# Attention of an encoder on one core: probabilities times values for 512 queries at a time

## The chip, the cores and the metric

The kernel runs on one core of a Trainium2 chip. The metric is device time in microseconds (us); the figure before is the median of 3 runs. The engines are named as in the profile: PE is the matrix engine (its weight loads are listed apart, as PEld), ACT the scalar engine, DVE the vector engine, POOL GpSimd, and SP issues the DMAs. Each engine takes its own instructions in program order, and the engines wait for each other through semaphores.

## The reference, cut to what matters

Two layers over 1024 tokens of width 1024. In each, attention with 8 heads stands beside a short convolution, and a projection, an MLP and a gate follow. The change is in attention:

```python
def one_block(args):
    qn_b, qr_b = args
    sc = (jnp.einsum('bqhd,bkhd->bhqk', qn_b, k_nope, preferred_element_type=jnp.float32)
          + jnp.einsum('bqhr,bkr->bhqk', qr_b, k_rope, preferred_element_type=jnp.float32))
    w = jax.nn.softmax(sc * scale, axis=-1)
    return jnp.einsum('bhqk,bkhd->bqhd', w.astype(v.dtype), v)
```

The last line, probabilities times values, is what the change recuts. The sum runs over 1024 keys; there are 64 value columns per head.

## The kernel before, in words

The kernel keeps float32 accuracy by splitting each operand into a high and a low part (`fp32r`) and adding products of the parts. Scores of 128 queries against 1024 keys are one step: a head has 8 steps s = 0 to 7. A step goes through three engines:

1. PE: `score.h.s`, six matmuls 512 wide (L1135 to L1137, tiles kh, hh, kl).
2. DVE: `least.h.s`, a reduction over the 1024 scores (L2386, nm).
3. ACT: `exp.h.s`, the exponential into pr (L1865).
4. PE: `turn.h.s.b`, b = 0 and 1, four transposes each of 128x128 (L1344, ps<-cst,pr) into PSUM bank 4 + b.
5. ACT: `high.h.s.b`, the copy into pth, the high part (L1653, pth<-ps).
6. DVE: `low.h.s.b`, the rest into ptl (L2393).
7. PE: `pv`, the product with the values vv (L1368 and L1369), from pth and ptl. Before, it is done for a quarter of the queries (two steps, 256 columns): `pv.h.G.part`, G = 0 to 3, where part 0 takes key chunks 0 to 3 and part 1 takes chunks 4 to 7. Each part is eight matmuls.

pth and ptl have a first index of 2, so that one quarter can be filled while the other is read.

Around this, PE also makes the next head's keys and values (`kv.1.t`, six matmuls), its queries (`q.1.t`, nine matmuls, on hh and wh or on hh and hl), turns its values by token (`v.1`, L1309) and makes the sums of squares of an output (`var`, L1174 and L1175). ACT and DVE copy, split and normalize these: on ACT `v`, `k` (accy and kh), `out` (of<-ps), `square` (sq<-of), `sq_high` (wh<-sq), `y` (yh<-of); on DVE `q` (tmp or xacc), `q_low` (hl), `sum` and `scale` (of), `sq_low` (wl<-sq,wh), `den` (dent), `y` (yl<-of,yh).

What sets the order is written out by hand: `ATT_PE`, `ATT_ACT` and `ATT_DVE` list the steps of one head for the three engines, and one pass over a list is called a round here. In a name like `turn.0.3.1` the first number is the head relative to the round: -1 is the head before, 1 the next. The change edits `ATT_PE` alone; the lists of ACT and DVE stand as they were. The parts of them that the text speaks of are these:

```python
ATT_ACT: ... exp.0.1 y.-1.0 v.1.0 k.1.0 last.7.1 exp.0.2 high.0.1.0 high.0.1.1 exp.0.3 v.1.1 k.1.1
out.-1.1 high.0.2.0 high.0.2.1 square.-1.1 sq_high.-1.1 unit.0 ...
ATT_DVE: ... sq_low.-1.1 least.0.4 low.0.3.0 low.0.3.1 den.0.0 least.0.5 unit.0 last.6.0 last.7.2
v_turned.1 least.0.6 q.1.0 low.0.4.0 low.0.4.1 scale.-1.1 least.0.7 q_low.1.0 low.0.5.0 low.0.5.1 q.1.1
sum.0.0 low.0.6.0 low.0.6.1 den.0.1 last.7.3 sq_low.0.0 least.1.0 q_low.1.1 low.0.7.0 low.0.7.1 y.-1.1
```

Steps named `last` are only in the round whose head is their first number. Waits that matter: a `turn` needs its `exp` and the `low` of the same b one step earlier (the bank is free then); `v.1` goes into bank 5 and waits for `low.0.3.1`; `kv.1.0` waits for the `ln` of an earlier output; `sq_low` waits for `sq_high`, and `q` on DVE for `q` on PE.

Of the kernel before, what the change touches and what calls it, by code (L numbers as in the profile page):

```python
# [29 lines left out]
HEADS, NOPE, ROPE, V_DIM = 8, 64, 32, 64  # L30
# [180 lines left out]
def steps(text):  # L211

    return [(word.split(".")[0],) + tuple(int(n) for n in word.split(".")[1:]) for word in text.split()]


ATT_PE = steps("""
turn.0.0.0 turn.0.0.1 score.0.2 kv.1.0 score.0.3 turn.0.1.0 turn.0.1.1 pv.-1.3.0 kv.1.1 pv.-1.3.1 turn.0.2.0
turn.0.2.1 score.0.4 pv.0.0.0 turn.0.3.0 turn.0.3.1 score.0.5 pv.0.0.1 var.-1.1 v.1 turn.0.4.0 score.0.6 q.1.0
turn.0.4.1 score.0.7 pv.0.1.0 pv.0.1.1 turn.0.5.0 turn.0.5.1 mix.0.0 q.1.1 turn.0.6.0 turn.0.6.1 mix.0.1
score.1.0 pv.0.2.0 turn.0.7.0 turn.0.7.1 mix.1.0 var.0.0 pv.0.2.1 score.1.1  # L220
""")

ATT_ACT = steps("""
# [243 lines left out]
def encoder(nc, x_in, w_units, w_head, p_in, gains, table, consts, out):  # L467
# [5 lines left out]
    def sb(name, shape, dt, where=ctx):  # L473
        return where.enter_context(nc.sbuf_tensor(name, shape, dt))

    def sem(name):
        return ctx.enter_context(nc.semaphore(name))
# [7 lines left out]
    with ctx:  # L485
# [41 lines left out]
        with ExitStack() as att:  # L527
# [19 lines left out]
            vv = sb("vv", [P, 2, 8, 3 * V_DIM], f32r, att)  # L547
            pth = sb("pth", [P, 2, 8, 256], f32r, att)
            ptl = sb("ptl", [P, 2, 8, 256], f32r, att)
# [23 lines left out]
        ps = ctx.enter_context(nc.psum_tensor("ps", [P, 8, HALF], f32))  # L573
# [98 lines left out]
        t_lo = sem("t_lo")  # L672
        pv_out = sem("pv_out")
# [227 lines left out]
        def step(L, h, s):  # L901

            return (L * HEADS + h) * STEPS + s
# [228 lines left out]
        def _(pe):  # L1132
# [82 lines left out]
            for L in range(DEPTH):  # L1215
# [37 lines left out]
                for n in range(0 if L else SLOTS, len(IN_OUTS) + 1):  # L1253
                    if n < len(IN_OUTS):
                        w, t = IN_OUTS[n]
# [89 lines left out]
                                                   pr[:, s % 2, (4 * b + c) * P:(4 * b + c + 1) * P], ident)  # L1345
                    last.then_inc(t_out, 1)

                def values(h, a, G, part):

                    H = L * HEADS + h  # L1350
                    if part == 0:
                        pe.wait_ge(t_lo, 2 * step(L, h, 2 * G + 2))
                    if (h, G, part) == (0, 0, 0):
                        pe.wait_ge(v_zero, L + 1)
                    if (G, part) == (0, 0):
                        if h + 1 < HEADS:
                            pe.wait_ge(k_lo, H * 2 + 4)
                            pe.wait_ge(v_f, H * 2 + 4)
                        else:
                            pe.wait_ge(o_ln, H * 2 - 1)  # L1360
                    if (G, part) == (2, 0):
                        if h + 1 < HEADS:
                            pe.wait_ge(q_f, H * 2 + 4)
                        else:
                            pe.wait_ge(o_ln, H * 2)
                    dst = ps[:, 6 + G // 2, (G % 2) * 256:(G % 2 + 1) * 256]
                    for c in range(4 * part, 4 * part + 4):
                        nc.tensor.matmul(dst, vv[:, a, c, V_DIM:3 * V_DIM], pth[:, G % 2, c, :], start=c == 0, stop=False)  # L1368
                        last = nc.tensor.matmul(dst, vv[:, a, c, 0:2 * V_DIM], ptl[:, G % 2, c, :], start=False, stop=c == 7)  # L1369
                    if part == 1:  # L1370
                        last.then_inc(pv_out, 1)

                def variances(h, a, t):

# [23 lines left out]
                def attend(h):  # L1398

                    for kind, o, *n in head_steps(h, ATT_PE):  # L1400
                        a, H = o % 2, L * HEADS + h
                        if kind == "turn":
                            transposes(o, *n)
                        elif kind == "score":
                            scores(o, a, *n)
                        elif kind == "kv":
                            if n[0] == 0:
                                if h:
                                    pe.wait_ge(o_ln, H * 2 - 1)
                                else:  # L1410
                                    pe.wait_ge(q_f, H * 2 + 2)
                            else:
                                pe.wait_ge(k_lo, H * 2 + 3)
                                pe.wait_ge(v_f, H * 2 + 3)
                            keys_and_values(o, a, n[0], 6)
                        elif kind == "v":
                            pe.wait_ge(t_lo, 2 * step(L, h, 3) + 2)
                            values_by_token(o, a, 0, 5)
                        elif kind == "q":
                            if n[0]:  # L1420
                                pe.wait_ge(q_f, H * 2 + 3)
                            elif h:
                                pe.wait_ge(o_ln, H * 2)
                            queries(o, a, n[0], 7)
                        elif kind == "pv":
                            values(o, a, *n)
                        elif kind == "mix":
                            mix_first(*n)
                        elif kind == "var" and (o, n[0]) != (HEADS - 1, 1):
                            variances(o, a, n[0])  # L1430
# [215 lines left out]
        def _(act):  # L1646
# [5 lines left out]
            def copy(dst, src, **more):  # L1652
                return nc.scalar.activation(dst, src, ACT.Copy, **more)  # L1653
# [108 lines left out]
            for L in range(DEPTH):  # L1762
# [4 lines left out]
                for n in range(8 if L else 0, len(IN_OUTS)):  # L1767
                    w, t = IN_OUTS[n]
# [100 lines left out]
                def high_of_transposed(h, s, b):  # L1869
                    G = s // 2  # L1870
                    act.wait_ge(t_out, 2 * step(L, h, s) + b + 1)
                    if (h, s, b) == (0, 0, 0):
                        act.wait_ge(tap, L * 12 + 12)
                    if (h, s, b) == (0, 2, 0):
                        act.wait_ge(mix_stored, L * MIX_STORED + 128)
                    if s % 2 == 0 and b == 0 and (G >= 2 or h):
                        act.wait_ge(pv_out, (L * HEADS + h) * 4 + G - 1)
                    copy(pth[:, G % 2, 4 * b:4 * b + 4, (s % 2) * P:(s % 2 + 1) * P],
                         ps[:, 4 + b, :].rearrange("p (c q) -> p c q", c=4)).then_inc(t_hi, 1)

# [51 lines left out]
                def attend(h):  # L1932
                    for kind, o, *n in head_steps(h, ATT_ACT):
                        a = o % 2
                        if kind == "high":
                            high_of_transposed(o, *n)
                        elif kind == "exp":
                            exponentials(o, *n)
                            if (o, n[0]) == (0, 1):
                                high_of_last_conv()  # L1940
                        elif kind == "v":
                            values_by_channel(o, a, n[0], 6)
                        elif kind == "k":
                            keys(o, a, n[0], 6)
                        elif kind == "v_turned":
                            values_by_token(o, a, 0, 5)
                        elif kind == "q":
                            queries(o, a, n[0], 7)
                        elif kind == "out":
                            outputs(o, a, n[0])  # L1950
                        elif kind == "square":
                            output_squares(o, a, n[0])
                        elif kind == "sq_high":
                            high_of_squares(o, n[0])
                        elif kind == "ln":
                            output_ln(o, a, n[0])
                        elif kind == "r":
                            output_factor(o, a, n[0])
                        elif kind == "y":
                            high_of_output(o, a, n[0])  # L1960
                        elif kind == "unit" and o + 2 < HEADS:
                            split_head(L, o + 2, a)
                        elif kind == "last":
                            split_unit(L, O_AT + n[0])
# [843 lines left out]
```

## Time and profile before

| what | before |
|---|---|
| time, median of 3 runs (2713.60 to 2713.67) | 2713.61 us |
| span of the profiled execution | 2712.5 us |
| PE busy | 2698.8 us, 99% |
| DVE busy | 2034.9 us, 75% |
| ACT busy | 1398.9 us, 52% |
| matmuls 256 wide of probabilities and values | 1024 |
| a round of attention, mean of six in the first layer | 34.4 us |

The profiled execution has a span of 2712.5 us from its first to its last instruction; the timed runs are 1.1 us above that. Matmuls are pipelined, and their durations in the profile overlap; what a matmul costs is the distance from its start to the start of the next. A row with x8 is a group of eight instructions merged; its time runs from the first start to the last end.

### The profile page before, as it was taken

To read this page: it belongs to the slowest core of one execution; us is meant where nothing else is said; L and a number is where in the kernel's file an instruction comes from. 1 tells how busy PE (TensorE), PEld (TensorE's weight loads), DVE (VectorE), ACT (ScalarE), POOL (GpSimd) and SP (SyncE) were. 2 spreads that over 40 slices of the span, in tenths; PEclk is the share of its full clock that TensorE was granted. 3 is DMA by queue.
4 is the path that set the end of the run, shared out by engine and by line. 5 is a ranking of instruction groups with operands and counts; after the bars stand their busy time and mean duration, and the time that the engine had idled before them with its cause. 6 is when DMAs were issued, how large, how long until landed. Compare 5 with 4: busy or idle time off the path is not lost.

```text
span 2712.5 us, 34671 instructions
## 1 busy us (share of the span) xinstructions
PE 2698.8 (99%) x12854; PEld 2242.9 (83%) x12854; DVE 2034.9 (75%) x2758; ACT 1398.9 (52%) x2401; POOL 302.7 (11%) x329
## 2 busy tenths in 40 slices
PE   9999999999999999999999999999999999999999
PEld 7888888888888888888888888888888888888886
DVE  5468888476787777798866788893867787777986
ACT  5337888564333333356634478884633333333464
POOL 0230000001111111110003200000011111111000
PEclk9999999999999999999999999999999999999999
DMA  4221112531111111133232111133311111111422
GB/s 166 78 72 37 34 34 76 181 109 71 62 47 55 39 58 51 63 117 117 86 119 73 60 41 34 29 132 131 140 45 49 63 47 55 39 55 55 148 94 78
DMA packets 85943, 206.19 MB, mean 76 GB/s; under 512 B 8976, under 2 KB 37776, under 8 KB 84752
## 3 DMA queue, kind: packets, MB, share of 16 engines
q1 hardware_dynamic: 85776, 203.97, 22.3%
q8 instruction: 103, 1.69, 0.3%
q14 instruction: 64, 0.52, 0.1%
HBM read 172.42 MB, written 31.52 MB: 75 GB/s over the span
## 4 chain that ended last, share of the span: by engine, by line
PE 96%; DVE 2%; ACT 1%; DMA 0%; issue 0%; SPq 0%; ACTq 0%
PE ps L1135 28%; PE ps L1137 28%; PE ps L1136 28%; PE ps L1344 4%; PE ps L1369 2%; PE ps L1368 2%; DVE nm L2386 1%; PE ps L1174 0%; PE ps L1175 0%; DVE ptl L2393 0%; PE ps L1309 0%; PE ps L1202 0%; ACT hh L1653 0%; DVE wl L2147 0%; PE ps L1160 0%; PE ps L1161 0%
## 5 line engine op out<-in xcount | busy, mean ns | idle before, releaser
L1135 PE MATMUL ps<-hh,wh 128*128 128x512 f32 x2160 | 847.9, 393 | 1.4 <-DVE hl L2183 1.3
L1137 PE MATMUL ps<-hh,wl 128*128 128x512 f32 x2160 | 840.8, 389 | 0.0
L1136 PE MATMUL ps<-hl,wh 128*128 128x512 f32 x2160 | 840.7, 389 | 0.0
L1653 ACT ACTIVATE wh<-raw 128x256 fp32r<-128x256 f32 (+2 forms) x510 | 319.2, 631 | 443.2 <-PE ps L1137 314.5
L2147 DVE TENSOR_TENSOR wl<-raw,wh 128x256 fp32r<-128x256 f32 (+2 forms) x510 | 379.6, 757 | 159.0 <-ACT wh L1653 158.6
L1135 PEld LDWEIGHTS ps<-hh,wh 128*128 128x128 f32 x2160 | 405.6, 188 | 89.1 <-issue 3.6
L1136 PEld LDWEIGHTS ps<-hl,wh 128*128 128x128 f32 x2160 | 405.6, 188 | 86.9 <-issue 3.6
L1137 PEld LDWEIGHTS ps<-hh,wl 128*128 128x128 f32 x2160 | 405.5, 188 | 84.5
L2574 DVE TENSOR_TENSOR xf<-xf,ps 128x1024 f32<-128x1024 f32 x280 | 337.4, 1214 | 35.9 <-PE ps L1137 34.7
L1135 PE MATMUL ps<-hx,wh 128*128 128x512 f32 x448 | 174.4, 389 | 0.5 <-DVE xf L2574 0.5
L1137 PE MATMUL ps<-hx,wl 128*128 128x512 f32 x448 | 174.3, 389 | 0.0
L1136 PE MATMUL ps<-hx,wh 128*128 128x512 f32 x448 | 174.3, 389 | 0.0
L2393 DVE TENSOR_TENSOR ptl<-ps,pth 128x512 fp32r<-128x512 f32 x256 | 163.8, 680 | 9.4 <-ACT pth L1653 8.8
L1653 ACT ACTIVATE pth<-ps 128x512 fp32r<-128x512 f32 x256 | 140.5, 595 | 48.2 <-PE ps L1344 45.0
L2386 DVE TENSOR_REDUCE nm<-ps 128x1 f32<-128x1024 f32 x128 | 155.4, 1214 | 1.4 <-PE ps L1137 1.1
L1865 ACT ACTIVATE pr<-ps,nm 128x1024 f32<-128x1024 f32 x128 | 142.8, 1115 | 14.2 <-DVE nm L2386 12.4
L2700 POOL TENSOR_TENSOR spare<-raw 128x256 f32<-128x256 f32 x56 | 43.2, 771 | 872.3 <-DMA raw<-w_units 872.3
L1344 PE MATMUL ps<-cst,pr 128*128 128x128 f32 x1024 | 138.3, 274 | 1.2 <-DVE ptl L2393 1.2
L1344 PEld LDWEIGHTS ps<-cst,pr 128*128 128x128 f32 x1024 | 116.2, 140 | 15.5 <-issue 4.0
L1368 PE MATMUL ps<-pth,vv 128*128 128x256 f32 x512 | 128.1, 284 | 0.0
L1369 PE MATMUL ps<-ptl,vv 128*128 128x256 f32 x512 | 127.2, 283 | 0.0
L1690 ACT ACTIVATE sq<-xf 128x512 f32<-128x512 f32 x168 | 103.1, 623 | 45.0 <-DVE accy L2177 19.8
(241 smaller groups left out, 4303.3 us busy)
## 6 DMA issues: line engine op xcount, KB each, us to landing
raw<-w_units SPq DMA_DIRECT2D x170, 512.0 KB, 3.4
raw<-w_units SPq DMA_DIRECT2D x112, 256.0 KB, 2.9
x_mid<-xf SPq DMA_DIRECT2D x4, 2048.0 KB, 7.9
xf<-x_mid SPq DMA_DIRECT2D x4, 2048.0 KB, 7.7
hh<-mix_hi SPq DMA_DIRECT2D x14, 512.0 KB, 6.1
hl<-mix_lo SPq DMA_DIRECT2D x14, 512.0 KB, 7.0
stage<-w_head SPq DMA_DIRECT2D x16, 320.0 KB, 3.3
mix_hi<-cyh SPq DMA_DIRECT2D x8, 512.0 KB, 2.6
```

What stands on the lines that cost most here:

```text
L1135: nc.tensor.matmul(dst, ah, bh, start=start, stop=False)
L1136: nc.tensor.matmul(dst, ah, bl, start=False, stop=False)
L1137: return nc.tensor.matmul(dst, al, bh, start=False, stop=stop)
L1344: last = nc.tensor.transpose(ps[:, 4 + b, c * P:(c + 1) * P], pr[:, s % 2, (4 * b + c) * P:(4 * b + c + 1) * P], ident)
L1368: nc.tensor.matmul(dst, vv[:, a, c, V_DIM:3 * V_DIM], pth[:, G % 2, c, :], start=c == 0, stop=False)
L1369: last = nc.tensor.matmul(dst, vv[:, a, c, 0:2 * V_DIM], ptl[:, G % 2, c, :], start=False, stop=c == 7)
L1653: return nc.scalar.activation(dst, src, ACT.Copy, **more)
L1865: nc.scalar.activation(pr[:, s % 2, :], ps[:, 2 * (s % 2):2 * (s % 2) + 2, :].rearrange("p b n -> p (b n)"), ACT.Exp, bias=nm[:, s % 2:s % ...
L2147: return V.tensor_tensor(dst, whole, high.bitcast(f32), ALU.subtract)
L2386: V.tensor_reduce(nm[:, s % 2:s % 2 + 1], ps[:, 2 * (s % 2):2 * (s % 2) + 2, :].rearrange("p b n -> p (b n)"), AX.X, ALU.min).then_inc(s_l ...
L2393: V.tensor_tensor(ptl[at], ps[:, 4 + b, :].rearrange("p (c q) -> p c q", c=4), pth[at].bitcast(f32), ALU.subtract).then_inc(t_lo, 1)
L2574: V.tensor_tensor(f, f, ps[:, bank:bank + 2, :], ALU.add if sign > 0 else ALU.subtract).then_inc(down_add, 1)
```

## The change

The product with the values is made for half of the queries (four steps, 512 columns) at a time. `pv.h.t.part` now has t = 0 and 1. There are 512 matmuls of 512 columns where there were 1024 of 256. pth and ptl keep their size, but both of their halves are now read by one product, so they are one buffer of a half and no longer two of a quarter. Part 0 waits for `low` of step 4t+3 with b = 0, part 1 for that with b = 1, and ACT waits with the first `high` of the next half (b = 0 and b = 1 each) until the part that reads the same chunks is done.

```diff
 ATT_PE = steps("""
-turn.0.0.0 turn.0.0.1 score.0.2 kv.1.0 score.0.3 turn.0.1.0 turn.0.1.1 pv.-1.3.0 kv.1.1 pv.-1.3.1 turn.0.2.0
-turn.0.2.1 score.0.4 pv.0.0.0 turn.0.3.0 turn.0.3.1 score.0.5 pv.0.0.1 var.-1.1 v.1 turn.0.4.0 score.0.6 q.1.0
-turn.0.4.1 score.0.7 pv.0.1.0 pv.0.1.1 turn.0.5.0 turn.0.5.1 mix.0.0 q.1.1 turn.0.6.0 turn.0.6.1 mix.0.1
-score.1.0 pv.0.2.0 turn.0.7.0 turn.0.7.1 mix.1.0 var.0.0 pv.0.2.1 score.1.1
+pv.-1.1.0 turn.0.0.0 pv.-1.1.1 turn.0.0.1 score.0.2 kv.1.0 score.0.3 turn.0.1.0 turn.0.1.1 kv.1.1 turn.0.2.0
+turn.0.2.1 score.0.4 turn.0.3.0 turn.0.3.1 score.0.5 var.-1.1 v.1 pv.0.0.0 turn.0.4.0 pv.0.0.1 turn.0.4.1 score.0.6
+q.1.0 score.0.7 turn.0.5.0 turn.0.5.1 mix.0.0 q.1.1 turn.0.6.0 turn.0.6.1 mix.0.1 score.1.0 turn.0.7.0 turn.0.7.1
+mix.1.0 var.0.0 score.1.1
 """)
...
-                def values(h, a, G, part):
+                def values(h, a, t, part):
...
-                    if part == 0:
-                        pe.wait_ge(t_lo, 2 * step(L, h, 2 * G + 2))
+                    pe.wait_ge(t_lo, 2 * step(L, h, 4 * t + 3) + part + 1)
...
-                    dst = ps[:, 6 + G // 2, (G % 2) * 256:(G % 2 + 1) * 256]
+                    dst = ps[:, 6 + t, :].rearrange("p (g n) -> p g n", g=2)
                     for c in range(4 * part, 4 * part + 4):
-                        nc.tensor.matmul(dst, vv[:, a, c, V_DIM:3 * V_DIM], pth[:, G % 2, c, :], start=c == 0, stop=False)
-                        last = nc.tensor.matmul(dst, vv[:, a, c, 0:2 * V_DIM], ptl[:, G % 2, c, :], start=False, stop=c == 7)
-                    if part == 1:
-                        last.then_inc(pv_out, 1)
+                        nc.tensor.matmul(dst, vv[:, a, c, V_DIM:3 * V_DIM], pth[:, :, c, :], start=c == 0, stop=False)
+                        last = nc.tensor.matmul(dst, vv[:, a, c, 0:2 * V_DIM], ptl[:, :, c, :], start=False, stop=c == 7)
+                    last.then_inc(pv_out, 1)
...
-                    if s % 2 == 0 and b == 0 and (G >= 2 or h):
-                        act.wait_ge(pv_out, (L * HEADS + h) * 4 + G - 1)
+                    if s % 4 == 0 and (s or h):
+                        act.wait_ge(pv_out, (L * HEADS + h) * 4 + s // 2 - 1 + b)
```

On PE, at the end of one round and the start of the next, the order before is this: the last score, then all eight transposes of step 0, then the next score and the keys and values (hh with hl in this head), without a value product between them.

```order
L1136 MATMUL ps<-kl,hh 128x512
L1137 MATMUL ps<-kh,hl 128x512
L1344 MATMUL ps<-cst,pr 128x128 x8
L1135 MATMUL ps<-kh,hh 128x512
```

At the same place of the changed kernel, all 16 value matmuls of the head before stand around the first four transposes.

```order
L1137 MATMUL ps<-kh,hl 128x512
L1367 MATMUL ps<-pth,vv 128x512
L1368 MATMUL ps<-ptl,vv 128x512
...
L1344 MATMUL ps<-cst,pr 128x128 x4
L1367 MATMUL ps<-pth,vv 128x512
L1368 MATMUL ps<-ptl,vv 128x512
...
L1344 MATMUL ps<-cst,pr 128x128 x4
L1135 MATMUL ps<-kh,hh 128x512
```

So two value parts now stand ahead of `turn.0.0.1`, `score.0.2` and `kv.1.0`. In the middle of a round, after `var.-1.1`, the order before is `v.1` (L1309), four transposes, a score (kh) and the next head's queries (hh with wh here).

```order
L1309 MATMUL ps<-cst,accy 128x64 x8
L1344 MATMUL ps<-cst,pr 128x128 x4
L1135 MATMUL ps<-kh,hh 128x512
```

In the changed kernel the same place reads so, with eight value matmuls in each of the two groups.

```order
L1309 MATMUL ps<-cst,accy 128x64 x8
L1367 MATMUL ps<-pth,vv 128x512
L1368 MATMUL ps<-ptl,vv 128x512
...
L1344 MATMUL ps<-cst,pr 128x128 x4
L1367 MATMUL ps<-pth,vv 128x512
L1368 MATMUL ps<-ptl,vv 128x512
...
L1344 MATMUL ps<-cst,pr 128x128 x4
L1135 MATMUL ps<-kh,hh 128x512
L1136 MATMUL ps<-kl,hh 128x512
```

Here too two value parts, and `turn.0.4.1` with them, have moved ahead of `score.0.6` and `q.1.0`.

## Rows read from the trace of the kernel before

**Rows 1.** The page: busy time by engine, and the granted clock in 40 slices.

```profile
PE 2698.8 (99%) x12854; PEld 2242.9 (83%) x12854; DVE 2034.9 (75%) x2758; ACT 1398.9 (52%) x2401; POOL 302.7 (11%) x329
...
PEclk9999999999999999999999999999999999999999
```

**Rows 2.** Stretches: six rounds of the first layer, from `turn.0.0.0` to `turn.0.0.0`.

```profile
254.84:461.14 206.30, 206.30 (x1309) 181.84 (x1308) 181.53 (x264) 174.85 (x313) 4.36 (x12) 1.00 0.11 29
```

**Rows 3.** Costliest groups: the high half of the value matmuls.

```profile
L1368 PE MATMUL ps<-pth,vv 128*128 128x256 f32 x512 | 128.1, 284 | 0.0
```

**Rows 4.** Timeline of PE in the second round: start, us, what.

```profile
270.97 0.71 PE L1309 MATMUL ps<-cst,accy 64*128 64x64 f32 x8
271.61 0.66 PE L1344 MATMUL ps<-cst,pr 128*128 128x128 f32 x4
...
273.50 0.39 PE L1135 MATMUL ps<-hh,wh 128*128 128x512 f32 x1
...
275.31 0.39 PE L1137 MATMUL ps<-hh,wl 128*128 128x512 f32 x1
275.55 0.60 PE L1344 MATMUL ps<-cst,pr 128*128 128x128 f32 x4
...
277.37 0.28 PE L1368 MATMUL ps<-pth,vv 128*128 128x256 f32 x1
...
279.30 1.04 PE L1344 MATMUL ps<-cst,pr 128*128 128x128 f32 x8
```

**Rows 5.** Timeline of ACT, second and third round.

```profile
265.92 0.62 ACT L1895 ACTIVATE sq<-of 64x512 f32<-64x512 f32 x1
266.57 0.63 ACT L1653 ACTIVATE wh<-sq 128x512 fp32r<-128x512 f32 x1
...
296.12 1.08 ACT L1653 ACTIVATE pth<-ps 128x512 fp32r<-128x512 f32 x2
297.08 1.13 ACT L1865 ACTIVATE pr<-ps,nm 128x1024 f32<-128x1024 f32 x1
...
298.17 0.62 ACT L1653 ACTIVATE accy<-ps 128x512 f32<-128x512 f32 x1
298.64 0.59 ACT L1653 ACTIVATE kh<-ps 64x512 fp32r<-64x512 f32 x1
299.26 0.59 ACT L1653 ACTIVATE of<-ps 64x512 f32<-64x512 f32 x1
299.88 1.09 ACT L1653 ACTIVATE pth<-ps 128x512 fp32r<-128x512 f32 x2
```

**Rows 6.** Timeline of DVE in the second round.

```profile
275.75 0.69 DVE L2372 SCALAR_TENSOR_TENSOR tmp<-ps,tab 128x512 f32<-128x512 f32 x1 [0.45 <-PE ps L1137]
276.35 1.28 DVE L2393 TENSOR_TENSOR ptl<-ps,pth 128x512 fp32r<-128x512 f32 x2
277.55 0.73 DVE L2418 SCALAR_TENSOR_TENSOR of<-of,gv,sq 64x512 f32<-64x512 f32 x1
278.21 1.21 DVE L2386 TENSOR_REDUCE nm<-ps 128x1 f32<-128x1024 f32 x1
279.34 0.67 DVE L2147 TENSOR_TENSOR hl<-tmp,hh 128x512 fp32r<-128x512 f32 x1
...
285.10 0.20 DVE L2401 STREAM_TRANSPOSE dent<-den 128x32 f32<-128x32 f32 x1
...
285.42 0.68 DVE L2147 TENSOR_TENSOR wl<-sq,wh 128x512 fp32r<-128x512 f32 x1
```

**Rows 7.** Timeline in the first round: PE waits for a `low` of DVE.

```profile
228.54 1.27 DVE L2393 TENSOR_TENSOR ptl<-ps,pth 128x512 fp32r<-128x512 f32 x2
...
229.36 1.23 PE L1344 MATMUL ps<-cst,pr 128*128 128x128 f32 x8 [0.16 <-DVE ptl L2393]
```

**Rows 8.** Timeline: `y` on ACT waits for a store of the part before.

```profile
288.96 0.67 DVE L2147 TENSOR_TENSOR yl<-of,yh 64x512 fp32r<-64x512 f32 x1
...
293.26 0.63 ACT L1653 ACTIVATE yh<-of 64x512 fp32r<-64x512 f32 x1 [1.16 <-DMA mix_lo<-yl]
```

More of the change, by code:

```diff
@@ L1346, in transposes @@
                     last.then_inc(t_out, 1)
-                def values(h, a, G, part):
+                def values(h, a, t, part):
                     H = L * HEADS + h
-                    if part == 0:
-                        pe.wait_ge(t_lo, 2 * step(L, h, 2 * G + 2))
-                    if (h, G, part) == (0, 0, 0):
+                    pe.wait_ge(t_lo, 2 * step(L, h, 4 * t + 3) + part + 1)
+                    if (h, t, part) == (0, 0, 0):
                         pe.wait_ge(v_zero, L + 1)
-                    if (G, part) == (0, 0):
+                    if (t, part) == (0, 0):
                         if h + 1 < HEADS:
@@ L1360, in values @@
                             pe.wait_ge(o_ln, H * 2 - 1)
-                    if (G, part) == (2, 0):
+                    if (t, part) == (1, 0):
                         if h + 1 < HEADS:
```

## Prediction

> **What bounds the kernel now.** I read the page first. PE is busy for 99% of the span, DVE for 75%, ACT for 52%, and the granted clock is in the top tenth in every slice, which is the upper of TensorE's two levels (2.4 GHz) [rows 1]. That says PE, on average. The change is in attention alone, so the stretches come next: six rounds of the first layer take 206.30 us, 34.4 us a round. PE never stops there, but DVE is busy 181.5 us (88%) and ACT 174.9 us (85%) [rows 2], against 75% and 52% over the whole span. So attention is a ring of three engines, nearly full, in which PE ends last. What a change there is worth depends on two numbers for a round: PE's own work, and the longest closed chain of waits through the three hand-written lists. A round cannot be shorter than either. Both follow from starts in the timelines.
>
> **Pitches, from start to start.** A 512-wide product: nine of them take 273.50 to 275.55, 0.228 us each; I take 0.23. A 256-wide value matmul: sixteen from 277.37 to 279.30, 0.1206 us each. `v.1`: 0.64. A half `turn` and a score: 275.55 to 277.37, 1.82, so the half turn alone 1.82 - 6 x 0.23 = 0.44 [rows 4]. The last product of a group reaches its reader 0.44 us after its own start (275.31 to 275.75), 0.21 more than its pitch [rows 4, 6]. ACT: `v` 0.47, `k` at most 0.62 (it may wait there; being the same operation as `v` I take 0.48), `out` 0.62, two `high` 0.96, `exp` 1.09, `square` 0.65, `sq_high` 0.63 and 0.05 to hand it on [rows 5]. DVE: every 512-wide step 0.60, `scale` 0.66, `least` 1.13, `den` 0.32, and 0.67 until a last `low` is done [rows 6]. From the end of a `low` to a waiting PE: the first of the pair is done at 228.54 + 0.67 = 229.21 and PE starts at 229.36, 0.15 [rows 7].
>
> **Part 1: half as many matmuls of twice the width.** Before, a head has 64 value matmuls, 64 x 0.1206 = 7.72 us of PE. After, it has 32; the trace has no value matmul of 512, so I bound it: below by the 0.228 of the products, above by two of 256, 0.241, if the two separate runs of 256 that it reads cost as much as two matmuls. I take 0.23: 32 x 0.23 = 7.36. The gain is 0.36 us a head, 5.8 us over 16 heads (bounds 0 and 6.8). The durations of 284 ns on the page are no help here, since matmuls overlap [rows 3]. The Trainium skill, "TensorE: Matmul & The Clock Gate", section "Back-to-back issue gap", gives N/2.4 + 2.5 ns for an isolated gap: 109.2 ns at 256 and 215.8 ns at 512, an estimate of 2.5 ns saved per pair and 1.3 us in all. Here the row shows 120.6 ns and about 230 ns, so the trace has more to save than the rule. PE's own work in a round becomes 34.4 - 0.36 = 34.0.
>
> **Part 2: what the order does to the chain.** The three lists of steps form this closed chain. I follow it once around in the changed kernel.
>
> A, on PE: `pv.-1.1.0` 1.84 (8 x 0.23), `turn.0.0.0` 0.44, `pv.-1.1.1` 1.84, `turn.0.0.1` and `score.0.2` 1.82, `kv.1.0` 6 x 0.228 = 1.37, tail 0.21: 7.52.
> B, on ACT, which waits for `kv.1.0`: `v` 0.47, `k` 0.48, `exp.0.2` 1.09, `high.0.1` twice 0.96, `exp.0.3` 1.09, `v` 0.47, `k` 0.48, `out.-1.1` 0.62, `high.0.2` twice 0.96, `square` 0.65, `sq_high` 0.68: 7.95.
> C, on DVE, which waits for `sq_high`: `sq_low` 0.60, `least.0.4` 1.13, `low.0.3.0` 0.60, `low.0.3.1` 0.67, to PE 0.15: 3.15.
> D, on PE, where `v.1` waits for `low.0.3.1`: `v.1` 0.64, `pv.0.0.0` 1.84, `turn.0.4.0` 0.44, `pv.0.0.1` 1.84, `turn.0.4.1` and `score.0.6` 1.82, `q.1.0` 2.05, tail 0.21: 8.84.
> E, on DVE, which waits for `q.1.0`: `q` 0.60, `low.0.4` twice 1.20, `scale` 0.66, `least.0.7` 1.13, `q_low` 0.60, `low.0.5` twice 1.20, `q` 0.60, `sum` 0.60, `low.0.6` twice 1.20, `den` 0.32, `sq_low` 0.60, `least.1.0` 1.13, `q_low` 0.60, `low.0.7.0` 0.67, to PE 0.15: 11.26. For `low.0.7.0` the next `pv.-1.1.0` waits, and the chain is closed.
>
> The sum is 38.7 us. Before, the same chain has no value part in it. It closes through `turn.0.0.0`, which waits for that `low` too, so A lacks 3.68; and in D `v.1`, `turn.0.4.0`, `score.0.6` and `q.1.0` follow each other, so D lacks two parts and a half turn, 4.12. That is 38.7 - 7.8 = 30.9 us, 3.5 under the 34.4 that PE takes, which is why it shows nowhere in the profile of before. The change puts all four value parts of a head into it. It then stands 4.7 us over PE's new 34.0, and DVE and ACT sit idle behind PE while value parts run, in a ring that had 12% to spare. The round grows by 38.7 - 34.4 = 4.3.
>
> **Part 3: one buffer.** The new waits of `high` on value parts have little to stop: `high.0.4.0` needs `pv.0.0.0`, which PE does before `turn.0.4.0` anyway, and `high` needs that turn. The same holds for b = 1 and for the next head. Cost zero; the cover is the order of PE itself. If it were gone, a wait here would be at most a part, 1.84.
>
> **The sum.** In each layer, the first head has no value parts ahead of it: its chain is 38.7 - 3.7 = 35.0, and one part stands before the next head's first turn, 36.9, +2.5. Six rounds at +4.3 are 25.8. The last head has no next keys or queries and several other steps in their place; I give it +4.3 too, with 0 and 7.8 (all moved work) as ends. A layer: 32.6; two: 65.2. Added to the span of 2712.5 this is 2777.7, and the timed runs lie 1.1 above the span: 2778.8. The pitches are those of runs without gaps; 0.1 us a round for small ones makes 2780. Nothing behind attention gives it back: MLP and projections wait for attention and keep PE busy as before.
>
> **The rivals.**
> *The gain alone (ends faster).* If the chain had 4.7 us more slack than I sum, PE would stay the bound and only part 1 counts: 2713.6 - 5.8 = 2707.8. It decides from the point where the chain is under 34.0. For it: PE does not wait once in these six rounds. Against it: each link is an order in a list or a wait in the code, and the pitches are the shortest that the rows show. Chance 0.04.
> *Half of it.* Some link is shorter than I read, by 1 to 3 us a round: 14 rounds or so, 2780 less 14 to 42, 2738 to 2766. Chance 0.10.
> *A store joins the chain.* `y.-1.0` on ACT stands before `v.1.0`, and its tile yh is free when the store of the part before has landed: 293.26 - (288.96 + 0.67) = 3.6 us after `y` on DVE [rows 8]. After the change `y.-1.1` follows `low.0.7.1` and ends about 0.8 us before the round's first turn; `y.-1.0` comes 0.44 + 1.84 + 0.64 + 0.48 + 1.09 = 4.5 after that turn (the turns, the part between them, the way to ACT, one `high`, one `exp`). So 5.3 - 3.6 = 1.7 us are left, less what the store waits in SP's queue behind the transfer of the sums. If that makes it 2 us too late, five heads in each layer pay: +20, 2800. Chance 0.07.
> *The clock falls.* PE now idles in pieces of up to about 1 us, 12% of a round. In the trace of before the granted clock stays at the upper level through PE's waits in the first round [rows 7, 1]. If it fell to 1.2 GHz for one round, its 34 us of PE work would take up to twice as long: 2814 and more. The Trainium skill, same page, section "What's actually happening", says that the clock is throttled unless PE is kept busy; by that rule a sparser PE is at risk. Chance 0.03.
> *The forecast.* Chance 0.76, with 2765 to 2798 as its own range: `k` at 0.62 twice a round adds 4 us, the 512-wide value matmul at 0.241 adds 5, the last head moves it by -9 to +7, and each handoff that is off by 0.05 moves it by less than 1 a link.
>
> **The numbers.** 2780. The range of 2758 to 2802 takes in most of the half case and the store. A difference of 0.2% (5.4 us) is about what can be told from no change. Slower by more: forecast, store, clock and half together, 0.95, of which I take off 0.01 for the unforeseen; the gain alone is just at the bound for faster, 0.04; 0.02 is left for the same.
>
> **What would show it.** In the profile after, the six rounds from the first `turn.0.0.0` to the seventh take 6 x 38.7 = 232 us, PE idles for 4.7 us of each (less in the listed waits, since modelled ends hide some 0.16 each time), and the releasers are `low` steps (ptl): before `v.1` (L1309) about 1 us, and before turns (L1344) and `pv.-1.1.0`. PE must wait for ACT hardly anywhere. Value matmuls have a pitch of 0.23. MLP stretches are unchanged. The forecast is wrong if PE idles at `v.1` and nowhere else, if the waits are put down to a DMA, or if the pitch of value matmuls is near 0.24 or above.

## The result, and the profile after

| | before | after |
|---|---|---|
| time, median | 2713.64 us | 2790.21 us (2789.11 to 2790.75) |
| ratio | | 1.0282 (1.0269 to 1.0295) |
| span of the profiled execution | 2712.5 us | 2787.3 us |

The change makes the kernel 76.6 us slower; 2780.0 was predicted, with 2758 to 2802 as the range. The page of the kernel after, its busy times, granted clock and the engines of the chain that ended last, and below it the line of that chain before:

```profile
PE 2726.1 (98%) x12342; PEld 2206.2 (79%) x12342; DVE 2036.7 (73%) x2758; ACT 1398.5 (50%) x2401; POOL 303.0 (11%) x329
...
PEclk9999999999999999999999999999999999999999
...
PE 85%; DVE 8%; ACT 5%; issue 2%; DMA 0%; SPq 0%; ACTq 0%
```

```profile
PE 96%; DVE 2%; ACT 1%; DMA 0%; issue 0%; SPq 0%; ACTq 0%
```

From [rows 1] to these lines the busy shares hardly move: PE was busy for 99% of the span and is for 98%. The chain that ended last does: it now runs through DVE and ACT for 13%, for 3% before. Busy shares alone give no reason for 75 us. Where they are is told by the first and the last transpose of probabilities (L1344) of each layer. The columns are least, median and largest ns, and first and last start. First the two layers before, then after:

```profile
L1344 PE MATMUL ps<-cst,pr x512: 270/272/329, 220.7 to 489.3; 128*128 128x128 f32 x171
L1344 PE MATMUL ps<-cst,pr x512: 270/273/329, 1563.9 to 1832.4; 128*128 128x128 f32 x171
```

```profile
L1344 PE MATMUL ps<-cst,pr x512: 270/273/447, 220.5 to 524.8; 128*128 128x128 f32 x171
L1344 PE MATMUL ps<-cst,pr x512: 270/273/303, 1601.0 to 1905.5; 128*128 128x128 f32 x171
```

Attention of the second layer took 268.5 us from first to last transpose and takes 304.5, +36.0; the first layer goes from 268.6 to 304.3, +35.7. From the last transpose of the second layer to the end of the span it was 880.1 us and is 881.8; behind the first layer's there are 1.7 us more as well, some 0.9 of them value work that now stands behind the last transpose. So attention has it all, and convolution, projections and MLP give nothing back. The six rounds that [rows 2] measured before:

```profile
256.69:493.74 237.05, 218.09 (x1117) 167.53 (x1116) 182.11 (x264) 174.88 (x312) 4.35 (x12) 1.00 0.09 25
```

They took 206.30 us and take 237.05: 39.5 a round for 34.4. DVE and ACT do the same work (182.1 and 174.9 us) in more time, and PE, which has no idle time in the row before, idles for 19 us. What it waits for in the whole kernel (us in total, times, longest):

```profile
PE ps L1344 <- DVE ptl L2391: 29.2, 41, 2.0
PE ps L1309 <- DVE ptl L2391: 9.5, 14, 0.8
PE ps L1174 <- DVE wl L2145: 3.7, 14, 0.3
PE ps L1367 <- DVE ptl L2391: 3.3, 15, 0.2
...
PE ps L1135 <- ACT pr L1863: 0.8, 2, 0.4
```

Nearly all is `low` (ptl), as said ahead. The chain can be followed through one round. PE, from the start of link A to the start of link D:

```profile
294.01 0.50 PE L1367 MATMUL ps<-pth,vv 128*128 128x512 f32 x1 [0.22 <-DVE ptl L2391]
294.35 0.39 PE L1368 MATMUL ps<-ptl,vv 128*128 128x512 f32 x1
...
295.73 0.40 PE L1368 MATMUL ps<-ptl,vv 128*128 128x512 f32 x1
295.96 0.60 PE L1344 MATMUL ps<-cst,pr 128*128 128x128 f32 x4
...
298.26 0.60 PE L1344 MATMUL ps<-cst,pr 128*128 128x128 f32 x4
...
309.36 1.23 PE L1344 MATMUL ps<-cst,pr 128*128 128x128 f32 x8 [1.34 <-DVE ptl L2391]
...
313.12 0.71 PE L1309 MATMUL ps<-cst,accy 64*128 64x64 f32 x8 [0.70 <-DVE ptl L2391]
```

ACT and DVE in the same round, where the chain passes to them:

```profile
301.66 0.60 ACT L1651 ACTIVATE accy<-ps 128x512 f32<-128x512 f32 x1 [0.29 <-PE ps L1137]
302.16 0.58 ACT L1651 ACTIVATE kh<-ps 64x512 fp32r<-64x512 f32 x1
302.76 1.11 ACT L1863 ACTIVATE pr<-ps,nm 128x1024 f32<-128x1024 f32 x1
...
309.39 0.63 ACT L1651 ACTIVATE wh<-sq 128x512 fp32r<-128x512 f32 x1
```

```profile
310.05 0.69 DVE L2145 TENSOR_TENSOR wl<-sq,wh 128x512 fp32r<-128x512 f32 x1 [0.24 <-ACT wh L1651]
...
320.04 1.22 DVE L2384 TENSOR_REDUCE nm<-ps 128x1 f32<-128x1024 f32 x1 [3.05 <-PE ps L1137]
322.10 0.69 DVE L2370 SCALAR_TENSOR_TENSOR tmp<-ps,tab 128x512 f32<-128x512 f32 x1 [0.84 <-PE ps L1137]
```

Each bracket is one engine that waits for the one before it in the chain. DVE alone idles for 3.05 and 0.84 us behind PE here, while the two value parts after `v.1` run. So the round grows although no engine has more work. The links against the prediction:

| link | predicted, us | measured, us |
|---|---|---|
| A, PE, 294.01 to 301.66 | 7.52 | 7.65 |
| B, ACT, to 310.05 | 7.95 | 8.39 |
| C, DVE, to 313.12 | 3.15 | 3.07 |
| D, PE, to 322.10 | 8.84 | 8.98 |
| E, DVE, to the next value part, 333.78 | 11.26 | 11.68 |
| sum | 38.7 | 39.8 |

### The profile page after: what moved, and what is told of

Same layout as the page of the kernel before. It is cut to its first block, busy times and chain, and to the rows that moved or that the text cites. A ratio compares the mean times of both kernels' runs of the same rounds, so it can differ in the third digit from the quotient of the medians.

```text
span 2787.3 us, 33647 instructions
## 1 busy us (share of the span) xinstructions
PE 2726.1 (98%) x12342; PEld 2206.2 (79%) x12342; DVE 2036.7 (73%) x2758; ACT 1398.5 (50%) x2401; POOL 303.0 (11%) x329
## 4 chain that ended last, share of the span: by engine, by line
PE 85%; DVE 8%; ACT 5%; issue 2%; DMA 0%; SPq 0%; ACTq 0%
PE ps L1135 26%; PE ps L1137 26%; PE ps L1136 26%; DVE ptl L2391 2%; PE ps L1367 2%; PE ps L1368 2%; DVE nm L2384 2%; ACT pr L1863 1%; ACT pth L1651 1%; PE ps L1344 1%; DVE wl L2145 1%; ACT wh L1651 1%; DVE hl L2145 1%; ACT sq L1893 0%; ACT of L1651 0%
## 5 line engine op out<-in xcount | busy, mean ns | idle before, releaser
L1344 PE MATMUL ps<-cst,pr 128*128 128x128 f32 x1024 | 151.7, 277 | 31.8 <-DVE ptl L2391 29.2
L1344 PEld LDWEIGHTS ps<-cst,pr 128*128 128x128 f32 x1024 | 114.7, 140 | 83.8 <-issue 69.7
L1367 PE MATMUL ps<-pth,vv 128*128 128x512 f32 x256 | 106.3, 415 | 3.3 <-DVE ptl L2391 3.3
L1135 PE MATMUL ps<-kh,hh 128*128 128x512 f32 x256 | 108.2, 423 | 1.1 <-ACT pr L1863 0.8
```

What stands on the lines that cost most here:

```text
L1135: nc.tensor.matmul(dst, ah, bh, start=start, stop=False)
L1344: last = nc.tensor.transpose(ps[:, 4 + b, c * P:(c + 1) * P], pr[:, s % 2, (4 * b + c) * P:(4 * b + c + 1) * P], ident)
L1367: nc.tensor.matmul(dst, vv[:, a, c, V_DIM:3 * V_DIM], pth[:, :, c, :], start=c == 0, stop=False)
```

## The experiments

Theories: **order** (the closed chain of PE's new order, as predicted), against **buffer** (one buffer in place of two makes `high` wait for value parts) and **width** (the 512-wide matmul costs more than two of 256). Rounds below are the distance from one `v.1` to the next in the first layer; it is 34.4 us before and 39.5 after. Where an expectation speaks of walking the lists, every engine is stepped through its list with the pitches of the rows and the waits of the code, and the length of a round is read from that.

### The order alone, narrow and with two buffers

The kernel before, with the parts where the change puts them. Nothing else is edited.

```diff
 ATT_PE = steps("""
-turn.0.0.0 turn.0.0.1 score.0.2 kv.1.0 ... pv.-1.3.0 kv.1.1 pv.-1.3.1 ...
+pv.-1.2.0 pv.-1.2.1 turn.0.0.0 pv.-1.3.0 pv.-1.3.1 turn.0.0.1 score.0.2 kv.1.0 ...
...
+var.-1.1 v.1 pv.0.0.0 pv.0.0.1 turn.0.4.0 pv.0.1.0 pv.0.1.1 turn.0.4.1 score.0.6 q.1.0 ...
```

> The kernel before (256-wide value matmuls, pth and ptl as two buffers of a quarter, its waits) with the changed kernel's order on PE: each value part of 512 columns is replaced by the two parts of the quarters that it covers. Chain theory (the order on PE puts the value parts into the closed chain of waits): PE makes the same stops as in the changed kernel. The chain that I can sum for this kernel closes one link later (pv.-1.3.0 waits for low.0.7.1) and comes to 37.3 us a round at least, walking all three lists with the pitches of the rows gives 38.7; so 2755 to 2790, likeliest 2780. Buffer theory (what costs is that one buffer of a half makes ACT wait for the value parts): with two buffers back, the time returns to about 2714, 2720 at most. Width theory (what costs is the 512-wide matmul over two runs): 2714 as well.

Measured: 2785.70 us (2784.68 to 2786.40), ratio 1.0264 (1.0249 to 1.028), rounds 39.25. Nothing wide and no shared buffer is in it, and the loss is 72.1 of the 76.6 us. Buffer and width fall as its cause. Its waits have the same shape as those after:

```profile
PE ps L1344 <- DVE ptl L2393: 29.7, 41, 2.0
PE ps L1309 <- DVE ptl L2393: 9.5, 14, 0.8
PE ps L1174 <- DVE wl L2147: 3.7, 14, 0.3
```

### One of the two moves alone

Only the parts at the start of a round are moved, and then only those of the middle.

```diff
+pv.-1.2.0 pv.-1.2.1 turn.0.0.0 pv.-1.3.0 pv.-1.3.1 turn.0.0.1 score.0.2 kv.1.0 ...
```

> The kernel before with only the last two quarters' value parts of the head before moved to the start of the round, around turn.0.0.0 (as in the changed kernel); the middle of the round stays as before. Chain theory: only 3.9 us of value parts join the chain; walking the lists gives 35.7 us a round instead of 34.4 and 2736 (2725 to 2750) in all. Buffer or width theory: 2714. If every moved part cost alike, without a threshold: half of the 77 us, 2752.

Measured: 2743.74 us (2742.53 to 2744.72), ratio 1.011 (1.0095 to 1.0125), rounds 35.8 and 36.5 in turn.

```diff
+var.-1.1 v.1 pv.0.0.0 pv.0.0.1 turn.0.4.0 pv.0.1.0 pv.0.1.1 turn.0.4.1 score.0.6 q.1.0 ...
```

> The kernel before with only the first two quarters' value parts moved behind v.1, around turn.0.4.0, and turn.0.4.1 ahead of score.0.6 (as in the changed kernel); the start of the round stays as before. Chain theory: 3.9 us of value parts and a half turn join the chain; walking the lists gives 36.6 to 37.3 us a round and 2752 to 2758 (2740 to 2770). Buffer or width theory: 2714. Start and middle together should come near the 70 to 77 us that both cost.

Measured: 2755.02 us (2754.26 to 2755.25), ratio 1.0151 (1.0136 to 1.0166), rounds 37.0 and 37.2. The two cost 30.2 and 41.4 us, 71.6 together, and 72.1 when made at once. If they lengthened two separate chains, the round with both would be the longer of the two, 37.1; it is 39.25. So with both made, both are links of one chain. But a chain of 30.9 with one move alone, 3.9 us of narrow parts at the start or 4.3 with the half turn in the middle, would have given 34.8 and 35.2, and 36.2 and 37.1 were measured. Of these 1.4 and 1.9 us the sum lacks 0.8 with both moves too (38.7 for 39.5). And if the two ate up the slack of one chain, together they would cost more than the sum of each alone, where they cost the same. So the slack of 3.5 us before is a sum and was not measured. Walking the whole lists had given 35.7 for the start and 36.6 to 37.3 for the middle. With one move alone the parts that stay at their old places (`pv.0.0.0` ahead of `turn.0.3.0`, and so on) stand in a way round too; the runs don't show which.

### Other orders of PE, the other lists as they are

In the changed kernel one part goes ahead of `v.1`, so that one link holds for `low.0.3.0` and not for `low.0.3.1`.

```diff
-... score.0.5 var.-1.1 v.1 pv.0.0.0 turn.0.4.0 pv.0.0.1 turn.0.4.1 ...
+... score.0.5 var.-1.1 pv.0.0.0 v.1 turn.0.4.0 pv.0.0.1 turn.0.4.1 ...
```

> The changed kernel with one step moved: pv.0.0.0 goes ahead of v.1 instead of behind it, so that PE does it in the time in which v.1 waits for low.0.3.1 (pv.0.0.0 itself waits for the low before that one). Chain theory: the chain loses the part of the 1.84 us that fits into PE's stop, 0.6 us a round: 2782 (2778 to 2786). Buffer and width theory: no change, 2790, since the same parts and waits remain.

Measured: 2783.81 us (2783.37 to 2784.43), ratio 1.0258 (1.0244 to 1.0272), rounds 39.07. Of the chain 0.4 us a round are gone, where 0.6 were expected of that link, and no more; buffer and width would have left it at 2790. The next one is the best order for PE that was found for the wide parts by walking the lists with the pitches of the rows, the lists of ACT and DVE untouched.

```diff
-... kv.1.1 turn.0.2.0 turn.0.2.1 score.0.4 turn.0.3.0 turn.0.3.1 score.0.5 var.-1.1 v.1 pv.0.0.0 turn.0.4.0 ... q.1.0
+... kv.1.1 score.0.4 turn.0.2.0 turn.0.2.1 score.0.5 turn.0.3.0 turn.0.3.1 var.-1.1 pv.0.0.0 q.1.0 v.1 turn.0.4.0 ...
```

> The changed kernel with the best order of PE's own list that I found by walking the lists, the lists of ACT and DVE untouched. Chain theory: PE's order alone can't take the value parts out of the chain, since all queries' turns of a half must come ahead of them and the fixed lists of ACT and DVE put the rest behind; 38.3 us a round, 2778 (2770 to 2786). If the changed order on PE were just badly chosen, a better one would bring it to 2720 or less.

Measured: 2782.52 us (2781.80 to 2783.06), ratio 1.0253 (1.0236 to 1.027). PE's list alone does not mend it.

### The lists of ACT and DVE alone

The changed kernel with PE's order as the change has it, and new lists for ACT and DVE.

```diff
 ATT_ACT = steps("""
-high.0.0.0 high.0.0.1 exp.0.1 y.-1.0 v.1.0 k.1.0 last.7.1 exp.0.2 high.0.1.0 high.0.1.1 exp.0.3 v.1.1 k.1.1
-out.-1.1 high.0.2.0 high.0.2.1 square.-1.1 sq_high.-1.1 ...
+high.0.0.0 y.-1.0 exp.0.1 out.-1.1 high.0.0.1 last.7.1 square.-1.1 sq_high.-1.1 v.1.0 k.1.0 exp.0.2 high.0.1.0
+...
+ln.-1.1 last.7.2 r.-1.1 exp.0.5 high.0.4.0 y.-1.1 out.0.0 high.0.4.1 square.0.0 sq_high.0.0 exp.0.6 ...
 ATT_DVE = steps("""
-scale.-1.0 low.0.0.0 low.0.0.1 ... y.-1.0 k.1.1 sum.-1.1 low.0.2.0 low.0.2.1 sq_low.-1.1 least.0.4 ...
+scale.-1.0 low.0.0.0 y.-1.0 sum.-1.1 low.0.0.1 ... low.0.4.0 sum.0.0 low.0.4.1 least.0.6 sq_low.0.0 y.-1.1 q.1.0 ...
+... low.0.7.0 low.0.7.1 den.0.1 least.1.1 q_low.1.1
```

> The changed kernel with its own order on PE and its one buffer, and only the lists of ACT and DVE put in another order, so that the steps on which PE's next stop waits come ahead of those that have time (found by walking the lists). Chain theory: the same matmuls, the same waits of high on value parts, but no closed chain above PE's work: 34.3 us a round, 2722 (2712 to 2735). Buffer theory: the waits of high on the value parts remain, so the time stays near 2790. Width theory: also near 2790.

Measured: 2769.29 us (2766.35 to 2770.57), ratio 1.0202 (1.0188 to 1.0216), rounds 37.6 to 39.6 from the second on: a miss. In the six rounds ACT's longest waits are for a DMA, which holds it five times:

```profile
ACT pth L1650 <- PE ps L1343: 20.1, 32, 1.4
ACT yh L1650 <- DMA mix_lo<-yl: 17.5, 5, 4.0
```

One such wait, on ACT and in SP's queue:

```profile
335.11 0.63 ACT L1650 ACTIVATE yh<-of 64x512 fp32r<-64x512 f32 x1 [3.36 <-DMA mix_lo<-yl]
```

```profile
328.93 1.26 SPq L1064 DMA_DIRECT2D sums<-dent  x4
331.08 0.47 SPq L1073 DMA_DIRECT2D sq<-sums  x1
331.59 0.60 SPq L1056 DMA_DIRECT2D mix_hi<-yh  x1
332.23 0.60 SPq L1056 DMA_DIRECT2D mix_lo<-yl  x1
```

The store of yl stands in SP's queue behind the transfer of the sums and was issued at 332.23, and `y.-1.0` on ACT, now early in the list, could start only at 335.11. `exp.0.1` and `k.1.0` stand behind it on ACT; in the same six rounds PE waits five times each for kl of DVE (8.3 us) and for pr of ACT (4.7 us). A part of the miss can be the clock: its mean over the profiled span is 0.995, by which some 14 of 2769 us of full clock are missing, less what PE would have waited anyway. The waits for the DMA are the rival "a store joins the chain". It is not in the changed kernel, where ACT waits for DMAs of weights only, but in a version of it that shortens the chain elsewhere. I had left SP's queue out of the walk. With it in, and `y` and `den` placed so that the store has time (`y.-1.1` on DVE behind `sq_low.0.0` of the round's end, `den.0.1` ahead of `low.0.6.0`):

```diff
 ATT_ACT = steps("""
+exp.0.1 y.-1.0 high.0.0.0 out.-1.1 high.0.0.1 last.7.1 square.-1.1 sq_high.-1.1 v.1.0 k.1.0 exp.0.2 high.0.1.0
+...
+ln.-1.1 r.-1.1 last.7.2 exp.0.5 y.-1.1 high.0.4.0 out.0.0 square.0.0 high.0.4.1 exp.0.6 q.1.0 high.0.5.0
 ATT_DVE = steps("""
+scale.-1.0 y.-1.0 low.0.0.0 sum.-1.1 low.0.0.1 ... low.0.4.0 sum.0.0 least.0.6 low.0.4.1 q.1.0 ...
+q.1.1 den.0.1 low.0.6.0 low.0.6.1 sq_low.0.0 y.-1.1 low.0.7.0 last.7.3 least.1.0 least.1.1 low.0.7.1 q_low.1.1
```

> Second try at the changed kernel with only the lists of ACT and DVE reordered. In the first try y on ACT waited up to 4.0 us for the store of the part before, which stands in SP's queue behind the transfer of the sums (den.0.1); with that store put into the walk, it gives the 37.5 us a round that the first try showed. This order gives the store its time. Chain theory: 34.5 us a round by the walk, 2724 (2716 to 2735), with PE's order and the one buffer of the changed kernel as they are. Buffer or width theory: near 2790. If the first try's shortfall had another cause than the store, this one stays at 2760 or more.

Measured: 2731.51 us (2730.07 to 2733.85), ratio 1.0066 (1.0052 to 1.008), rounds 34.9. PE executes the changed order to the letter, with one buffer and wide matmuls, and 58.7 of the 76.6 us are back. So the loss belongs to neither PE's order nor ACT's and DVE's by itself: it is what the three lists cost together. The last round, where several steps are others, loses still; the longest wait there is 2.83 us for ptl. The mean granted clock of 0.998 can be some 5 us of the 17.9 that are left.

### All three lists, wide and narrow

The changed kernel with three new lists, and the same lists with 256-wide parts and two buffers, to read the width where PE ends last.

```diff
 ATT_PE = steps("""
-pv.-1.1.0 turn.0.0.0 pv.-1.1.1 turn.0.0.1 score.0.2 kv.1.0 score.0.3 ... v.1 pv.0.0.0 turn.0.4.0 pv.0.0.1 ... q.1.0
+pv.-1.1.0 kv.1.0 score.0.2 pv.-1.1.1 turn.0.0.0 turn.0.0.1 score.0.3 ... q.1.0 pv.0.0.0 v.1 turn.0.4.0 score.0.6 pv.0.0.1 ...
 ATT_ACT = steps("""
+exp.0.1 v.1.0 y.-1.0 last.7.1 k.1.0 out.-1.1 high.0.0.0 high.0.0.1 exp.0.2 square.-1.1 sq_high.-1.1 ...
 ATT_DVE = steps("""
+scale.-1.0 least.0.2 y.-1.0 k.1.0 last.7.1 sum.-1.1 low.0.0.0 low.0.0.1 least.0.3 sq_low.-1.1 ... low.0.7.0 ... low.0.7.1
```

> The changed kernel with all three lists (PE, ACT, DVE) in another order, found by walking the lists. Chain theory: PE is the bound again, with 0.36 us less work a head than before: 33.9 us a round by the walk, where the kernel before walks at 34.3; 2708 (2704 to 2715), faster than both. Buffer or width theory: 2760 or more.

> Control for the run with all three lists in another order: the same ACT and DVE lists and the same places on PE, but with the 256-wide value matmuls and two buffers of the kernel before. If what makes the wide one faster than before is the width, this one lies 5 to 6 us above it, at 2713 (2709 to 2718); if it is the order, both are alike.

Measured: wide 2712.47 us (2712.20 to 2713.42), ratio 0.9995 (0.9986 to 1.0004), rounds 34.2: inside the expected 2704 to 2715, but not the expected gain on the kernel before. Narrow 2716.49 us (ten of eleven executions lie from 2716.10 to 2717.15; one took 11415.86, for which no reason is on record), ratio 1.001 (1.0001 to 1.0019), rounds 34.5. At these lists the width, with the one buffer, is worth 4.0 us by the times, and 0.3 us a round. The page of the wide one:

```profile
PE 2694.1 (99%) x12342; PEld 2210.1 (82%) x12342; DVE 2035.0 (75%) x2758; ACT 1399.2 (52%) x2401; POOL 299.9 (11%) x329
...
PE 95%; DVE 4%; ACT 1%; issue 0%; DMA 0%; SPq 0%; ACTq 0%; DVEq 0%
```

A second set of lists, with the two transposes of a step drawn apart and `kv.1.0` first in the round:

```diff
 ATT_PE = steps("""
+kv.1.0 pv.-1.1.0 turn.0.0.0 score.0.2 pv.-1.1.1 turn.0.0.1 turn.0.1.0 score.0.3 kv.1.1 turn.0.1.1 turn.0.2.0 ...
```

> The changed kernel with all three lists reordered once more, from the order that gave 2712.5, with the store in the walk. Chain theory: 33.9 us a round as there, and 1 to 1.5 us less per layer in the first and the last head: 2710 (2707 to 2713).

Measured: 2713.76 us (2713.36 to 2714.28), ratio 0.9999 (0.999 to 1.0008): outside the expected 2707 to 2713, and no gain. Its rounds are 34.1, 0.25 under those before, which would be 3.5 us in 14; it is not seen in the time. Its longest waits on PE (us in total, times, longest):

```profile
PE ps L1343 <- DVE ptl L2390: 2.7, 4, 0.8
PE ps L1343 <- ACT pr L1862: 1.9, 2, 1.0
PE ps L1134 <- DVE xacc L2369: 1.7, 2, 0.9
```

They happen four, two and two times in the whole kernel, so in single rounds; that the lists serve the first and the last round less well is the likely reason, and it was not tested. No version beats the kernel before by more than can be told; the best of them is level with it.

## Why the prediction was right, step by step

- **What bounds: right.** A round is the longer of PE's own work and the closed chain. The change makes the chain longer, with the six rounds in full: 237.05 us for 232 predicted. The stops are where they were said to be: ptl before `v.1` (0.70 us for 1), before turns and before `pv.-1.1.0`, and ACT hardly holds PE (0.8 us in all). PE's idle time in the profile is 3.2 us a round, not 4.7; as foretold, modelled ends hide a part of each stop. What is not shown is the other half of the argument, that the chain had 3.5 us of slack before: one move alone costs more than that allows.
- **Part 2, the mis-sized term.** The chain was summed to 38.7 and takes 39.5 on average, so the six rounds cost 30.7 and not 25.8 a layer. Of the 1.05 us missing in the round shown, B has 0.44 and E 0.42. In B, `k` costs 0.60 and 0.62 to the next start where I took 0.48, although [rows 5] had 0.62 for it; I put that down to a wait, because the operation's name is the same as for `v`. That is 0.26 of the 0.44, and the own range of the forecast had named it (4 us, for 0.62 twice a round). Most of the rest of B is 0.15 at the square, which starts 1.11 us after the pair of pth, for 0.96. Neither is a fixed price of its shape. In the round before this one, after the change, the same `k.1.0`, with the same tiles, takes 0.48:

```profile
262.90 0.58 ACT L1651 ACTIVATE kh<-ps 64x512 fp32r<-64x512 f32 x1
263.38 1.10 ACT L1863 ACTIVATE pr<-ps,nm 128x1024 f32<-128x1024 f32 x1
```

Here the exponential starts 0.10 us before the end of `k`, and at 302.76 above 0.02 behind it. The square comes 0.97 after the pair in that round. What decides between the two was not tested, nor what the small pieces of E are.
- **First and last head: right.** +2.1 and +2.5 for the two first heads (2.5 predicted); 4.5 for each last one (4.3), 2.9 of it up to the last transpose and 1.7 behind it.
- **Part 1, the width.** Predicted 5.8 us with bounds of 0 and 6.8; the pair of runs with the same lists measures 4.0. The pitch is as taken: the seven from 294.35 to the transpose at 295.96 take 1.61 us, 0.230 each. Under the changed order the width gains nothing at all: the wide kernel is 4.5 us slower than the narrow one with that order. A fall of the clock explains about 1.7 of it (last section). For the rest there is a reading that no run tested: the first wide part needs both steps of its half, so it waits for `low.0.7.0` in 15 rounds (3.3 us in the waits), while in the narrow kernel the first quarter needs only earlier steps and starts right behind the score:

```profile
332.66 0.39 PE L1137 MATMUL ps<-kh,hl 128*128 128x512 f32 x1
332.89 0.28 PE L1368 MATMUL ps<-pth,vv 128*128 128x256 f32 x1
```

- **Part 3, the buffer at zero: right as far as tested.** Order and narrow parts alone give 72.1 of 76.6 us, and the second run with new lists keeps the one buffer and comes to within 17.9 us of the kernel before; with all lists, it is level. No wait of `high` for a value part has a row of its own in the waits of after.
- **The rivals.** The gain alone (2707.8) did not come; the version with all lists gets near it at 2712.47. Half of it did not come; the error had the other sign. The store is not in the change and did appear in the first run with new lists. The clock fell once, for a few us and not for a round.

## What to carry to other kernels

Before moving work within one engine's list, close the chain: from the moved step through every engine's queue back to itself, at the pitches of the rows, and compare the sum with the busiest engine's own work. A full engine that never waits can hide a chain with little slack, and here 7.8 us of matmuls moved into one with, by the sum, at most 3.5 to spare. When only a part of the work moves, other ways round count too, and the one chain summed too little. When the work must move, the lists of the other engines have to move with it, DMA queues among them; take the pitch of an operation from its own rows, at each place where it stands, not from another with the same name.

## What the runs showed of the hardware that was not expected

**The same stop, and another clock.** At the end of attention in the first layer PE stops for 2.01 us, and right afterwards it runs at the lower level, 1.2 GHz. The kernel after, timeline and then the stretch:

```profile
502.99 1.68 PE L1344 MATMUL ps<-cst,pr 128*128 128x128 f32 x8 [2.01 <-DVE ptl L2391]
...
505.32 0.63 PE L1137 MATMUL ps<-kh,hl 128*128 128x512 f32 x1
505.75 0.63 PE L1135 MATMUL ps<-kh,hh 128*128 128x512 f32 x1
```

```profile
503.00:507.00 4.00, 4.00 (x15) 3.25 (x16) 2.94 (x5) 3.30 (x7) 0.53 (x1) 0.57 1.00 402
```

The narrow kernel with the changed order, at its own copy of the place:

```profile
501.08 1.23 PE L1344 MATMUL ps<-cst,pr 128*128 128x128 f32 x8 [2.02 <-DVE ptl L2393]
```

```profile
503.00:507.00 4.00, 3.38 (x20) 2.47 (x19) 3.63 (x6) 3.15 (x7) 0.00 (x0) 1.00 1.03 422
```

In the first the pitch of a 512-wide matmul is 0.43 us in place of 0.23 and the mean granted clock of those 4 us is 0.57, which is 1.7 us of full clock lost; in the second a stop as long leaves the clock at 1.00. So does the stop at the same place of the second layer in the kernel after itself, where the 512-wide matmul keeps its 0.23:

```profile
1883.75 1.23 PE L1344 MATMUL ps<-cst,pr 128*128 128x128 f32 x8 [2.01 <-DVE ptl L2391]
...
1885.05 0.39 PE L1136 MATMUL ps<-kl,hh 128*128 128x512 f32 x1
1885.28 0.40 PE L1137 MATMUL ps<-kh,hl 128*128 128x512 f32 x1
```

With the start alone moved, the clock fell behind both stops of 2.02 us. In the first run with new ACT and DVE lists alone it fell after a stop of 1.63 us (at 380.2), not after an equal one (at 303.5), and was below 1.00 in eight stretches of 10 us over the kernel. What decides was not found, so here a stop of 1.6 to 2 us is to be counted as a risk of 1.7 us on top. The Trainium skill, "TensorE: Matmul & The Clock Gate", section "What's actually happening", says the clock is throttled unless PE is kept busy; the first case agrees, and the second shows that a stop of 2.02 us alone is not enough to bring it down. The same page, section "Wait — 56ns, not 53.3ns?", gives 426.7 ns from start to start for 512 columns at the lower level and 215.7 ns at the upper: the trace agrees with the first (0.43) and not with the second (0.23).

**A first matmul is dearer.** After a stop, and after transposes, the next 512-wide matmul holds PE for 0.31 to 0.34 us and not 0.23 (294.01 to 294.35). Behind transposes it is so without a stop too (296.32 to 296.64 is 0.32). Each such place costs this kernel about 0.1 us.

**Rounds alternate.** After, rounds of odd and even heads take 39.25 and 39.77 us by the first transpose. It lies in links B and E (8.12 and 11.43 for odd heads, 8.39 and 11.68 for even ones). In B it is the two pitches named above: 0.48 or 0.60 for `k.1.0`, 0.97 or 1.11 for the pair of pth ahead of the square. The cause is open.
